# A four-layer block in one launch: the opening's split, ScalarE's table sets, and a few orders of work

## The reference, cut to what matters

```python
h = rmsnorm(x, pre_norm[0]); x = x + rmsnorm(mamba2_mixer(h, ssm_w_in, ..., ssm_w_out), post_norm[0])
h = rmsnorm(x, pre_norm[1]); x = x + rmsnorm(swa_sink_mixer(h, att_w_in, ..., att_w_out), post_norm[1])
h = x
h = h + conv_pool_mixer(rmsnorm_2(h, norm_mix_g[0]), cp_w_in, ..., cp_w_out)
h = h + swiglu_ffn(rmsnorm_2(h, norm_ffn_g[0]), w1[0], w3[0], w2[0])
h = h + hgrn2_mixer(rmsnorm_2(h, norm_mix_g[1]), hg_w_in, ..., hg_w_out)
h = h + swiglu_ffn(rmsnorm_2(h, norm_ffn_g[1]), w1[1], w3[1], w2[1])
return rmsnorm_2(h, final_g)
# rmsnorm: x * rsqrt(mean(x*x) + EPS) * w.  hgrn2 per head h: o * rsqrt(mean(o*o) + EPS), then * gn_g
# mamba2: softplus(dt), exp of decays within chunks of 128 tokens, chunk products C.B, states carried on
```

## Time and profile before

| | us |
|---|---|
| median of 3 runs | 1868.53 |
| the profiled execution | 1868.22 |
| its span, first to last instruction | 1866.2 |
| TensorE matmul busy | 1837.4 (98%) |
| VectorE busy | 1074.1 (58%) |
| GpSimd busy | 892.1 (48%) |
| ScalarE busy | 574.8 (31%) |
| granted TensorE clock, mean | 0.996 of full speed |

### The profile page before, as it was taken

The page is one execution under the profiler, slowest core; times in us unless marked ns, Lnnn a source line. Parts: engine busy times, 40 slices in busy tenths (PEclk is TensorE's granted clock), DMA queues, the critical chain, the costliest instruction groups (busy, mean ns, idle before and its releaser), DMA issues.

```text
span 1866.2 us, 25091 instructions
## 1 busy us (share of the span) xinstructions
PE 1837.4 (98%) x9700; PEld 1469.8 (79%) x9700; DVE 1074.1 (58%) x1673; ACT 574.8 (31%) x1036; POOL 892.1 (48%) x902
## 2 busy tenths in 40 slices
PE   8999999999999999999999999999999999999998
PEld 7788888788777777488888888877777788888887
DVE  6888888984887667653333313357878633333212
ACT  4544445512344331331111100236655421111001
POOL 6444454444533435255555555543432455555553
PEclk9999999999999999999999999999999999999999
DMA  9867767667754579488888888875652788888875
GB/s 237 174 154 154 162 144 154 158 160 152 162 127 102 118 168 227 119 182 188 195 195 191 184 191 201 200 168 132 136 125 69 159 194 191 190 199 194 185 169 133
DMA packets 217263, 309.89 MB, mean 166 GB/s; under 512 B 22782, under 2 KB 171450, under 8 KB 217146
## 3 DMA queue, kind: packets, MB, share of 16 engines
q0 software_dynamic: 42912, 148.65, 46.3%
q1 hardware_dynamic: 170970, 155.93, 27.0%
q10 hardware_dynamic: 3264, 3.71, 0.7%
HBM read 153.12 MB, written 2.10 MB: 83 GB/s over the span
## 4 chain that ended last, share of the span: by engine, by line
PE 89%; DVE 6%; ACT 2%; DMA 1%; issue 1%; POOL 1%; SPq 0%; DVEq 0%; POOLq 0%; ACTq 0%
PE gp L774 23%; PE gp L776 22%; PE gp L775 22%; PE gp L746 2%; PE gp L748 2%; PE gp L747 2%; PE mp L1179 1%; PE gp L714 1%; PE mp L1076 1%; PE gp L715 1%; PE gp L721 1%; DVE m_xs L1995 1%; DMA wl<-stage 1%; PE mp L944 1%; PE mp L1040 1%
## 5 line engine op out<-in xcount | busy, mean ns | idle before, releaser
L665 POOL TENSOR_SCALAR wh<-stage 128x1024 fp32r<-128x1024 f32 (+2 forms) x298 | 347.0, 1164 | 849.4 <-PE gp L776 686.3
L774 PE MATMUL gp<-hh,wh 128*128 128x512 f32 x1504 | 602.0, 400 | 3.1 <-POOL wh L665 1.5
L775 PE MATMUL gp<-hh,wl 128*128 128x512 f32 x1504 | 586.3, 390 | 0.0
L776 PE MATMUL gp<-hl,wh 128*128 128x512 f32 x1472 | 574.7, 390 | 0.0
L666 POOL TENSOR_SCALAR wl<-stage 128x1024 fp32r<-128x1024 f32 (+2 forms) x298 | 352.6, 1183 | 0.0
L774 PEld LDWEIGHTS gp<-hh,wh 128*128 128x128 f32 x1504 | 282.7, 188 | 74.2 <-issue 18.0
L775 PEld LDWEIGHTS gp<-hh,wl 128*128 128x128 f32 x1504 | 283.0, 188 | 57.0 <-issue 1.4
L776 PEld LDWEIGHTS gp<-hl,wh 128*128 128x128 f32 x1472 | 276.6, 188 | 59.7
L669 POOL DMA_DIRECT2D wl<-stage x298 | 264.6, 888 | 94.7 <-POOL wl L666 85.8
L2461 DVE TENSOR_TENSOR val<-gp,rstd 128x512 f32<-128x512 f32 x44 | 30.4, 692 | 202.9 <-PE gp L776 202.9
L2330 DVE TENSOR_TENSOR xT<-gp,xT 128x512 f32<-128x512 f32 x31 | 21.4, 689 | 195.2 <-PE gp L776 190.3
(11 more groups left out here) (391 smaller groups left out, 2786.8 us busy)
## 6 DMA issues: line engine op xcount, KB each, us to landing
wl<-stage POOLq DMA_DIRECT2D x263, 512.0 KB, 5.4
stage<-ffn_w SPq DMA_DIRECT2D x120, 512.0 KB, 4.4
stage<-ssm_w_in SPq DMA_DIRECT2D x32, 512.0 KB, 4.5
stage<-hg_w_in SPq DMA_DIRECT2D x32, 512.0 KB, 4.3
stage<-ssm_w_in SPq DMA_DIRECT2D x32, 256.0 KB, 4.9
stage<-ssm_w_out SPq DMA_DIRECT2D x16, 512.0 KB, 3.7
stage<-att_w_in SPq DMA_DIRECT2D x14, 512.0 KB, 4.5
stage<-cp_w_in SPq DMA_DIRECT2D x12, 512.0 KB, 5.6
```

The source lines that it names most:

```text
L665: pool.tensor_scalar(wh[:, s, part], stage[:, s, part], 1.0, 1.0, ALU.mult, ALU.mult).then_inc(hi_done, 1)
L774: pe.matmul(bank[:, :], wvh[:, cols], hi(kk), start=start, stop=False)
L775: pe.matmul(bank[:, :], wvl[:, cols], hi(kk), start=False, stop=False)
L776: mm = pe.matmul(bank[:, :], wvh[:, cols], lo(kk), start=False, stop=stop)
```

## The change

- GpSimd makes the low parts of the third and fourth half of all (the second halves of the first two units) by subtraction; the negation and the adding transfer of these two are gone, TensorE and SP wait for `early_split` instead.
- In the opening x is turned into three banks, and the low part of x is taken from the bank, not from `xT`; a bank is used again when the low part is made (`split_done`).
- For the last k of a lead of two units, the first unit's products all come ahead of the second unit's.
- The four chunk products of group 0 come one granule (12 products) later; the next slot runs one granule less.
- ScalarE loads a table set that holds both ln and exp (`natural_log_exp_and_others`) for the roots, and keeps track of what is loaded. Before, the set with ln alone was loaded and then, by the compiler, one for exp.
- At the start of conv and pool, GpSimd makes the second half of the third unit only when all low parts of the activations are made.
- In the recurrence's fourth pair, ScalarE's root goes ahead of the two logs, and VectorE's value of the head ahead of the two scans.

```diff
@@ -601,10 +601,10 @@
                 if q >= HALVES:
-                    if s < EARLY and q < 2 * HALVES:
+                    if q < 2 * HALVES:
                         sp.wait_ge(early_split, EARLY + s + 1)
                     else:
-                        sp.wait_ge(lo_landed[s], 16 * (q // HALVES - (s < EARLY)))
+                        sp.wait_ge(lo_landed[s], 16 * (q // HALVES - 1))
                 ka, kb = rows_of(u, i)
@@ -658,14 +658,21 @@
                         pool.wait_ge(split_done, split0["y"] + 2)
+                    if (before, half) == (phases["cp"][0] + 1, 0):
+                        pool.wait_ge(split_done, split0["pre2"] + KT)
                     if (u, i) == (phases["hg_out"][1] - 2, 0):
...
                 pool.tensor_scalar(wh[:, s, part], stage[:, s, part], 1.0, 1.0, ALU.mult, ALU.mult).then_inc(hi_done, 1)
+                if q < HALVES:
+                    pool.wait_ge(hi_done, q + 1 - EARLY)
+                    pool.tensor_tensor(wl[:, s, part], stage[:, s, part], wh[:, s, part].bitcast(F32),
+                                       ALU.subtract).then_inc(early_split, 1)
+                    continue
                 pool.tensor_scalar(wl[:, s, part], stage[:, s, part], -1.0, 1.0, ALU.mult,
                                    ALU.mult).then_inc(neg_done, 1)
-                pool.wait_ge(neg_done, q + 1 - EARLY)
+                pool.wait_ge(neg_done, q + 1 - HALVES)
                 pool.dma_start(wl[:, s, part], stage[:, s, part], accum_op=ALU.add).then_inc(lo_landed[s], 16)
@@ -676,9 +683,11 @@
+                elif q < HALVES:
+                    pe.wait_ge(early_split, EARLY + q + 1)
...
-                    pe.wait_ge(lo_landed[q % HALVES], 16 * (q // HALVES + 1 - (q % HALVES < EARLY)))
+                    pe.wait_ge(lo_landed[q % HALVES], 16 * (q // HALVES))
@@ -700,33 +709,35 @@
-                    for u in range(u0, u0 + lead):
...
+                    lead_units = list(range(u0, u0 + lead))
+                    for part in ([lead_units] if k < KT - 1 else [[u] for u in lead_units]):
+                        for u in part:
+                            wvh, wvl = weights_at(u, k)
...
+                            for m, t in enumerate(units[u].tiles):
+                                if k == 0 and t >= 4:
+                                    pe.wait_ge(bank_read[t % 4], t // 4)
+                                cols = slice(m * P, (m + 1) * P)
+                                bank = gp[t % 4]
+                                pe.matmul(bank[:, :], wvh[:, cols], hi(k), start=(k == 0), stop=False)
+                                pe.matmul(bank[:, :], wvl[:, cols], hi(k), start=False, stop=False)
...
+                        pe.wait_ge(split_done, split(k) + 1)
+                        for u in part:
+                            wvh, _ = weights_at(u, k)
+                            for m, t in enumerate(units[u].tiles):
+                                cols = slice(m * P, (m + 1) * P)
@@ -830,10 +841,10 @@
-                if k >= 2:
-                    pe.wait_ge(x_tile, k - 1)
+                if k >= 3:
+                    pe.wait_ge(split_done, split0["pre0"] + k - 2)
...
-                    mm = pe.transpose(mp[1 + k % 2][:, c * P:(c + 1) * P], xin[:, c, k * P:(k + 1) * P], ident)
+                    mm = pe.transpose(mp[1 + k % 3][:, c * P:(c + 1) * P], xin[:, c, k * P:(k + 1) * P], ident)
@@ -884,7 +895,7 @@
-                def turn_and_cb(g):
+                def turn_x_b(g):
@@ -902,7 +913,12 @@
+
+                def chunk_products(g):
+                    xg = xs[:, g % 2]
...
+                    if g:
+                        pe.wait_ge(h_ready, g)
@@ -961,7 +977,10 @@
-                            turn_and_cb(p)
+                            turn_x_b(p)
+                            if p == 0:
+                                run(gran, 1)
+                            chunk_products(p)
@@ -978,7 +997,7 @@
-                            run(gran, 2)
+                            run(gran, 1 if (g, slot) == (1, 1) else 2)
@@ -1324,9 +1343,17 @@
-            def load_ln():
-
-                act.preload_act_table_set("natural_log")
+            loaded = [None]
+
+            def load_table(name):
+
+                if loaded[0] != name:
+                    act.preload_act_table_set(name)
+                    loaded[0] = name
+
+            def load_root():
+
+                load_table("natural_log_exp_and_others")
@@ -1335,7 +1362,9 @@
-                load_ln()
+                if r:
+                    loaded[0] = None
+                load_root()
@@ -1408,6 +1437,7 @@
+                load_table("natural_log")
@@ -1733,10 +1770,10 @@
                             elif s == 3 and n:
+                                head_root(n - 1)
                                 if p == late_pair and k == 11:
...
                                     log_f(p, 1)
-                                head_root(n - 1)
                             elif s == 5 and n:
@@ -1828,7 +1864,8 @@
-                    dve.scalar_tensor_tensor(hl[:, k, :], xT[:, k, :], prm[:, col:col + 1], hh[:, k, :].bitcast(F32),
+                    src = xT[:, k, :] if v else mp[1 + k % 3][:, :]
+                    dve.scalar_tensor_tensor(hl[:, k, :], src, prm[:, col:col + 1], hh[:, k, :].bitcast(F32),
@@ -1860,7 +1897,7 @@
-                dve.tensor_copy(xT[:, k, :], mp[1 + k % 2][:, :]).then_inc(x_tile, 1)
+                dve.tensor_copy(xT[:, k, :], mp[1 + k % 3][:, :]).then_inc(x_tile, 1)
@@ -2618,10 +2655,10 @@
                             elif s == 4 and n:
+                                head_value(n - 1)
                                 if p == late_pair and k == 12:
...
                                     scan(p, 1)
-                                head_value(n - 1)
                             elif s == 5:
```

45 lines of the change are left out of this document (16 added, 29 removed).

## The result

The changed kernel took 1855.82 us (median of 4 runs, 1854.69 to 1857.83), the kernel before 1868.44 beside it (4 runs, 1868.3 to 1868.77). The ratio is 0.9935, 95% interval 0.9923 to 0.9947: 12.6 us less, where 10.5 were forecast. Five more runs had a median of 1856.79 (ratio 0.9937, 0.9924 to 0.9949). The profiled execution took 1856.57, its span is 1854.7. TensorE is busy 1832.7 us of it where it was 1837.4, and idle 22.0 where it was 28.8: of the 11.5 us that the span lost, 6.8 are idle time and 4.7 are work done faster or closer together.

The account below looks back on a forecast made before the run. TensorE, busy 98% of the span, was taken as the bound, so only its waits count. Savings of 2.0 + 1.4 + 0.9 + 2.0 + 1.5 + 1.4 + 1.3 = 10.5 us gave 1858.0; range 1854.8 to 1863.5.

Parts of the forecast that it names:

- Opening: Third and fifth tile: low parts from PSUM and subtraction remove waits of 1.48 and 1.25; 2.0 us taken of 2.73.
- Chunk products: Group 0's chunk products: twelve products and a dropped table load cover the wait for the last silu; 1.4 us saved.
- Attention: Start of attention: the 0.77 wait goes, then a transfer limits; its chain starts four products earlier, so 0.9 us saved.
- Conv and pool: Start of conv and pool: holding GpSimd removes the 1.42 wait, dropping the table load the 0.77; 2.0 us taken of 2.19.
- Rival B: Conv and pool: the held half lands too late, a new wait of about 2.2 eats the gain; 1860.0 us, chance 12%.
- Recurrence: Fourth pair: root and value go first, saving 1.5 us of the 1.79 wait; the clock not falling saves 1.4 more.
- rival C: Recurrence: the clock falls all the same, as TensorE's small products stay; 1859.4 us, chance inside the forecast's 58%.
- End of the recurrence: Last root: the table load of 1.28 before its exp goes; 1.3 us saved, 1.0 of the 2.27 wait stays.
- Rival A: SSM stage: VectorE, nearly full, becomes the bound and the early gains are handed back; 1861.4 us, chance 14%.
- Rival D: Opening: the low part still stands behind GpSimd, now 2.5 us at a time; 1860.0 us, chance 7%.
- Rival F: Recurrence's end: the wait at 1468.68 goes whole, 1.0 us more saved; 1857.0 us, chance 2%.
- Rival E: Opening: a late low part or fourth half makes the clock fall, costing 10.8 us; slower, 1870.8 us, chance 3%.

Follow-up runs that it names:

- one of its halves alone: The kernel before with only the low parts of x taken from PSUM over three banks: 1868.38 us, ratio to before 1.0004.

## Why the prediction was right

1856.57 for the profiled execution against 1857.7; the median 2.2 below the 1858.0 (that of all nine runs 1.4), inside the range. Every stage of the sum gained, but the recurrence not by the way that was forecast, and that the sum came so near is in part luck. The sizes:

- **Opening**, 2.0 forecast, 3.1 to 3.5 measured, above the upper end of 2.73. The small waits of 0.2 to 0.4 that the step subtracted did not come, and 0.3 was hidden in a gap too small to be listed: the third tile's first product came 0.67 behind the turn ahead of it and comes 0.35 behind it now. The prices of the low part (0.7) and of the subtraction (2.5 against 2.72) were right. What the step did not see is that its two halves are not a sum: neither alone can be told from nothing. Writing 1.48 + 1.25 was right for both together only.
- **A removed wait is worth more than its idle time.** The end of a product is shown 0.39 after its start, while the next starts 0.23 after it, so each wait hides 0.16 of spacing, and the first product behind a wait is spaced 0.31, 0.08 more. That is some 0.25 a wait. Five waits went whole (18.39, 24.04, 64.07, 693.57, 701.88) and none of a size came before the recurrence: 1.2 us that no term had, and that lie in the measured gains of the three stages. The gain at 696, 1.71 for an idle time of 1.42, and at 70, 1.70 for 1.43, show it best.
- **Chunk products**, 1.4 forecast, 1.7 gained at that place, of which the move is 1.2.
- **Attention**, 0.9 forecast, 1.1 measured, 1.1 by undoing it. As forecast the transfer took over (5.50 us from issue to landing).
- **Conv and pool**, 2.0 forecast, 2.7: the hold 1.7, the table load 0.8 to 1.0. Rival B's margin of 0.3 was in truth none (the transfer landed 0.14 ahead of a product that came 0.17 late), so that B stayed away by luck. And the forecast took the collision of addition and GpSimd for fixed, where a shift of 1.5 us takes it away.
- **Recurrence**, 1.5 for the wait and 1.4 for the clock, 1.2 measured for both. This is where the prediction failed. The chain did get 1.8 us shorter (the gain goes from 9.5 to 11.2 at 1408.46). But its lower end had named what came then ("GpSimd meets the levels' products instead"): 1.27 and 1.26 instead of 0.42, a wait of 1.21 where none had stood, and 1.00 where 0.58 had, a wait that the prediction had left out. So the idle time fell from 2.68 to 2.52, and the wait's term is 0.2 and not 1.5. The clock fell all the same, as rival C had it; yet it stood at 0.50 for some 3.4 us (1401.8 to 1405.2) instead of 6.8 (1409.3 to 1416.1), and the same work between these two products took 1.1 us less outside the waits, of the 1.4 forecast. The reason given, that the clock does not fall with the wait nearly gone, was not tested: the waits did not go, and with these same waits the clock fell in four traces and stayed up in two.
- **End of the recurrence**, 1.3 forecast, 0.8: the load went, but the value's second product now takes 1.26 beside GpSimd at 1453.04 instead of about 0.7.
- **Rival A** (handed back): the gain of 4.8 at 70 is 4.9 at 440. **Rival D**: low parts at 0.73 to 0.75. **Rival F**: the wait at the end is 1.56. **Rival E** needed a wait longer than those of before, at a low part or the fourth half, to let the clock fall in the opening; the changed kernel has none, but one of its halves alone has (2.06, with the clock at 0.50). It lost 2.9 us by that clock, where E had 10.8, as the clock was back at 1.00 from 30.2 on. That the clock can fall earlier, at the first tiles, was no rival; it did in four of the profiled kernels.

So the sum came near because errors cancelled. By place, the terms that were too small (opening 1.1, chunk products 0.3, attention 0.2, conv and pool 0.7, and 0.8 of clock at a norm that no term had) outweighed by 1.0 the recurrence, too large by 1.7, and its end, by 0.5. The spacing behind removed waits (1.2) is inside the opening's, the chunk products' and conv and pool's.

## What to carry to other kernels

Before counting two removed waits as a sum, ask for each one alone what TensorE meets when it arrives earlier: here the low part and the weights each hid behind the other, and half of the change would have measured as nothing. Here VectorE's instructions with both operands in SBUF were two to seven times as long beside GpSimd (1.34 against 0.68, 3.03 against 0.42). Giving one an operand in PSUM, or holding GpSimd until it is done, was worth the whole wait, where the two did fall together and the held transfer still landed in time. When a chain becomes shorter, list what the other engine does at the new time, not at the old one.

## What was not expected of the hardware

- The clock behind one and the same pattern of waits is 1.00 in one execution and 0.50 in another, at four places of up to 1.6 us each. I take it for the cause of the 4 us spread of the changed kernel, whose waits in the recurrence are the same to 0.01 us in both of its profiled executions; the other executions left no trace, so this is not shown. A wait of 2.59 at the first product left it at 1.00, and one of 1.76 was followed by 0.50.
- VectorE's instruction that starts 0.04 or 0.44 us ahead of GpSimd ends 0.5 us after GpSimd's second instruction all the same (2.95 and 3.37 instead of 0.74 and 0.68).
- A table load takes 1.28 us and the next activation starts 0.01 to 0.02 later. In the fourth pair, four of them where the changed kernel has two cost TensorE 4.0 us.
